# Identity products on TensorE between the first modulation products and at the end of two blocks

## What is computed

```python
def decoder_layer(x, c, S0, u_prev, k_buf, v_buf, pos0, lw):
    mods = (jax.nn.silu(c) @ lw['w_ada'] + lw['b_ada']).reshape(c.shape[0], N_ADA, 1, D_MODEL)
    sh1, sc1, gt1, sh2, sc2, gt2, sh3, sc3, gt3 = [mods[:, i] for i in range(N_ADA)]
    x = x + 0.5 * gt1 * swiglu(modulate(x, lw['norm_ffn1'], sh1, sc1), lw['ffn1_w_gu'], lw['ffn1_w_down'])
    m, st = parallel_heads(modulate(x, lw['norm_mix'], sh2, sc2), u_prev, S0, k_buf, v_buf, pos0, lw)
    x = x + gt2 * m
    x = x + 0.5 * gt3 * swiglu(modulate(x, lw['norm_ffn2'], sh3, sc3), lw['ffn2_w_gu'], lw['ffn2_w_down'])
    return x, st
```

## Time and profile before

| | |
|---|---|
| median of three runs | 2444.17 us |
| time of the profiled execution | 2454.07 us |
| its span, first to last instruction | 2452.3 us |
| TensorE busy | 2363.1 us, 96% of the span |
| VectorE, ScalarE, GpSimd busy | 1107.3, 386.8, 536.3 us |
| mean granted TensorE clock | 0.98 |

### The profile page before, as it was taken

The page is one execution under the profiler, slowest core; times in us unless marked ns, Lnnn a source line. Parts: engine busy times, 40 slices in busy tenths (PEclk is TensorE's granted clock), DMA queues, the critical chain, the costliest instruction groups (busy, mean ns, idle before and its releaser), DMA issues. The chain is left out here.

```text
span 2452.3 us, 50615 instructions
## 1 busy us (share of the span) xinstructions
PE 2363.1 (96%) x21666; PEld 2245.2 (92%) x21666; DVE 1107.3 (45%) x2449; ACT 386.8 (16%) x890; POOL 536.3 (22%) x278
## 2 busy tenths in 40 slices
PE   7899999999999989999989899999999999999997
PEld 5899999999999989888568885999999999999997
DVE  4624443334444364434576665147333444433344
ACT  4100000000000132434621123131000000000003
POOL 3312121212212032111331124313212212121111
PEclk9999999999999999989799999999999999999999
DMA  9232221111011142100320002332111011111102
GB/s 339 86 104 89 82 86 52 50 35 51 17 51 51 45 114 60 36 18 27 113 64 5 4 4 72 108 104 69 52 34 51 17 51 51 51 51 34 51 9 73
DMA packets 162810, 151.22 MB, mean 62 GB/s; under 512 B 21616, under 2 KB 142113, under 8 KB 162264
## 3 DMA queue, kind: packets, MB, share of 16 engines
q1 hardware_dynamic: 162136, 146.75, 19.2%
q10 hardware_dynamic: 144, 2.23, 0.2%
q0 software_dynamic: 384, 0.07, 0.0%
HBM read 137.98 MB, written 11.34 MB: 61 GB/s over the span
## 5 line engine op out<-in xcount | busy, mean ns | idle before, releaser
L516 PE MATMUL bank<-hh,f_up_hi 128*128 128x368 f32 (+1 forms) x2064 | 677.3, 328 | 1.9 <-POOL hl L440 1.0
L518 PE MATMUL bank<-hh,f_up_lo 128*128 128x368 f32 (+1 forms) x2064 | 675.3, 327 | 0.0
L517 PE MATMUL bank<-hl,f_up_hi 128*128 128x368 f32 (+1 forms) x2064 | 674.4, 327 | 0.0
L1291 DVE TENSOR_TENSOR f_prod<-f_silu,bank 128x368 f32<-128x368 f32 x132 | 70.2, 532 | 763.0 <-PE bank L518 758.2
L531 DVE SCALAR_TENSOR_TENSOR x<-bank,mods,x 128x368 f32<-128x368 f32 (+1 forms) x544 | 306.1, 572 | 199.7 <-PE bank L518 186.9
L516 PEld LDWEIGHTS bank<-hh,f_up_hi 128*128 128x128 f32 x2064 | 387.6, 188 | 7.4 <-issue 7.3
L517 PEld LDWEIGHTS bank<-hl,f_up_hi 128*128 128x128 f32 x2064 | 387.8, 188 | 0.0
L518 PEld LDWEIGHTS bank<-hh,f_up_lo 128*128 128x128 f32 x2064 | 387.7, 188 | 0.0
L995 POOL TENSOR_TENSOR f_up_lo<-f_up_raw,f_up_hi 128x2048 fp32r<-128x2048 f32 x44 | 203.2, 4619 | 768.5 <-DVE f_up_hi L1278 768.5
L516 PE MATMUL bank<-f_a_hi,f_dn_hi 128*128 128x368 f32 (+1 forms) x1056 | 347.0, 329 | 0.8 <-DVE f_scratch L534 0.8
L518 PE MATMUL bank<-f_a_hi,f_dn_lo 128*128 128x368 f32 (+1 forms) x1056 | 345.5, 327 | 0.0
(11 more groups left out here) (385 smaller groups left out, 2894.2 us busy)
## 6 DMA issues: line engine op xcount, KB each, us to landing
f_up_raw<-in_ffn_w_gu SPq DMA_DIRECT2D x88, 512.0 KB, 5.0
f_dn_raw<-in_ffn_w_down SPq DMA_DIRECT2D x22, 1024.0 KB, 7.4
late<-in_w_ada SPq DMA_DIRECT2D x12, 1024.0 KB, 4.9
ada<-in_w_ada SPq DMA_DIRECT2D x16, 512.0 KB, 10.9
w_in_raw<-in_w_in SPq DMA_DIRECT2D x16, 512.0 KB
gates<-in_w_ada SPq DMA_DIRECT2D x8, 1024.0 KB, 7.4
x_in<-in_x_prompt SPq DMA_DIRECT2D x8, 512.0 KB, 8.0
ada<-in_w_ada SPq DMA_DIRECT2D x4, 1024.0 KB, 9.9
```

The costliest lines, as they stand in the source:

```text
L516: pe.matmul(out, wh, rh, start=(n == 0), stop=False)
L517: pe.matmul(out, wh, rl, start=False, stop=False)
L518: ins = pe.matmul(out, wl, rh, start=False, stop=(n == last))
L1291: dve.tensor_tensor(prod[u % 2][:, 0:n], silu[u % 2][:, 0:n], k.psum[2 * (u % 2) + 1][:, 0:n], ALU.mult).then_inc(up_free, 1)
```

## The change

A helper issues products of the 128x128 float32 identity with itself into a PSUM bank that nothing reads afterwards. It is called with 8, 8, 10 and 4 products between the four first modulation products and the spreads, with 16 at the end of the first feed-forward's block, and with 20 at the end of the recurrence block. One wait is added ahead of the first modulation product, for VectorE's copy out of the bank that the products write.

```diff
--- before.py
+++ after.py
@@ -509,6 +509,13 @@
                 self.spread(pe, t)
 
 
+def keep_busy(pe, k, bank, n):
+
+    ident = k.c("ident")
+    for _ in range(n):
+        pe.matmul(bank[:, 0:P], ident, ident, start=True, stop=True)
+
+
 def three_passes(pe, out, pairs):
 
     last = len(pairs) - 1
@@ -621,11 +628,16 @@
             turn(j)
         norm.means(pe, 1)
         pe.wait_ge(self.c_done, 1)
+        pe.wait_ge(self.x_high, self.NX - 1)
         self.half_product(pe, 0, 0)
+        keep_busy(pe, k, k.psum[3], 8)
         self.half_product(pe, 0, 1)
         norm.spread(pe, 0)
+        keep_busy(pe, k, k.psum[3], 8)
         self.half_product(pe, 0, 2)
+        keep_busy(pe, k, k.psum[3], 10)
         self.half_product(pe, 0, 3)
+        keep_busy(pe, k, k.psum[3], 4)
         norm.spread(pe, 1)
         ada.turn(pe, 0, self.turned)
         pe.wait_ge(self.par_done, 1)
@@ -1200,6 +1212,7 @@
                     three_passes(pe, out[:, 0:TW], [(hi[:, c], lo[:, c], k.hh[:, c, 0:TW], k.hl[:, c, 0:TW]) for c in range(KD)]
                                  ).then_inc(win.mm_done, 1)
                 mix.means(pe, 2)
+                keep_busy(pe, k, k.psum[6], 16)
 
             if first:
                 pe.sem_inc(late.used, 4)
@@ -2895,6 +2908,7 @@
             for m in range(PAIRS):
                 ins = pe.transpose(k.psum[1][0:HD, P * m:P * m + P], state[:, m], ident)
             ins.then_inc(wkv_turned, 1)
+            keep_busy(pe, k, k.psum[0], 20)
 
         @block.vector
         def _(dve):
```

## The result

The changed kernel took 2452.29 us, the median of 13 runs (2447.23 to 2459.93); the kernel before, timed beside it, 2443.51 us, the median of 13 (2438.44 to 2454.71). The ratio is 1.0033, 95% interval 1.0021 to 1.0044: 8.1 us slower, between 5.1 and 10.8. The time forecast was 2448.0 in a range of 2441 to 2454, so the range holds it; "no difference that can be measured", the likeliest case of the forecast, is wrong.

What follows compares the result with a forecast made beforehand. Long stages were taken as bound by TensorE's products, so only three gaps at half clock could pay: -0.3 + 2.2 + 1.9 = +3.8 us, 2444.17 becoming 2448.0 us, range 2441 to 2454.

Steps and rivals of the forecast that it cites:

- no difference that can be measured: Whole kernel: a change under 0.2% (4.9 us) either way, given a chance of 0.59.
- spare time: Both block ends: TensorE drains before GpSimd, by 0.92 us at the first and 2.43 us at the recurrence's.
- first end: First feed-forward's block end: 16 products delay the block by 2.7 us, a kept clock may save 0.9; taken as +2.2 us.
- recurrence end: Recurrence block's end: 20 products delay it by 3.6 us, output projection at full clock returns 1.7; +1.9 us.
- price of a product: All three places: one identity product takes 0.225 us at full clock, 0.453 at half, judged from the spreads.
- the first place: Kernel start, 8, 8, 10 and 4 products: clock kept up, VectorE gets the turn 0.3 us sooner; -0.3 us.
- the refund: Kernel start: fourth modulation product, spread and turn run at full clock; the fourth takes about 1.07 us, not 1.94.
- the three places don't depend on that: Whole kernel: the profiled execution, 9.9 us above the median, still gives the median's shift, +3.8 us.
- The bound of +1.7: Kernel start: cost in an execution whose clock would not have fallen, turn at 37.56 against 35.85; +1.7 us.
- Rival 1: All three places: products do not hold the clock and cost 0.453 us each; +17.8 us, 2462, chance 0.10.
- Rival 2: Recurrence's end alone stays at half clock until its block is over; sum +9.0 us, 2453.2, chance 0.17.
- Rival 3: All three places: products are cheap, near a transpose's 0.09 us; sum -3.8 us, 2440.4, chance 0.13.

Runs made afterwards that it cites:

- within the slack: Kernel before plus three identity products at the first block's end and four at the recurrence's, none at the start: ratio 0.9992.
- more products: The full change with 56 and 60 products at the two block ends in place of 16 and 20: ratio 1.0089 to the kernel before.

## Why the prediction was right or wrong

**The mechanism at the two block ends was right.** The prediction named who drains last, the spare time of 0.92 and 2.43 us, and that the 16 products push the pause they were to fill. All are in the profile after. Forecast and measured: first end +2.2 and +2.5, recurrence end +1.9 and +1.6. The experiments within the slack and with more products bear the rule out on both sides of the spare time. That the first end costs 0.3 more than forecast fits the spare time, which was taken from the execution with the most of it.

**The price of a product was right, that of a group was left out.** At full clock a product takes 0.225 us as forecast, but each group of them about 0.18 more. In the three groups ahead of the fourth modulation product that is 0.5 us.

**The step that failed is the first place, "-0.3 us, all on the path".** It measures +2.0 in the stage, +2.6 from the first modulation product to the turn. Two things went wrong in it. The overrun was larger by the groups: in the profile after the turn starts at 38.17 and not at 37.56. Above all, the refund was taken from one execution, in which the fourth modulation product ran at half clock, as if that were every execution's: "the three places don't depend on that" is the sentence that does not hold. In six of the seven profiles without products the turn came 9.92 to 10.54 us after the first modulation product, in the one used for the forecast 12.63. The bound of +1.7, for an execution in which the clock had not fallen, described what most executions do, also those in which the clock falls at the second product, and it was dismissed with "the trace shows the other case". So the sum should have been nearer 6 than 3.8, and past the 4.9 us that can be told from nothing.

**The rivals.** Rival 1 (the products do not hold the clock) is out: the clock stood at 1.00 through 24.9 to 38.9 us in the change, and TensorE's 56 products in 12.77 us kept the pace. Its sum was too small besides: it counts 0.453 us only from the ten products on; with the first sixteen at that price too, by the same steps, the turn would start near 47 us and not at 42.5. The argument against it is sound, though the clock column of the earlier trace rows reads 1.00 in both microseconds and its counts are not starts: four transposes start in the first and ten in the second, 0.21 and 0.11 us apart. Rival 2 gave the time that came, +9.0, but not for its reason: the clock climbed within the 20 products in the profile after, and they took 5.87 us, not nine (6.35 and 6.53 in the other two profiles with 20). Rival 3 (products near 0.09 us) is out, with 0.225.

**The range and the chances.** The range held the time because it took in rival 2, whose mechanism did not occur: that is luck and not the sum. The chance of 0.36 for slower was low for the reason above.

## What to carry to other kernels

Products that only keep TensorE's clock up are free exactly where TensorE waits and somebody else sets the end of that wait; count their price against the spare time, and before a point where all engines meet read who drains last first. What they can return is only the half-speed part of the work that follows, and if that work then waits for another engine, the pause has merely moved. A refund that rests on the clock must be read from several executions: one profile shows one of its cases.

## What was not expected of the hardware

- The pauses that drop the clock are not the same from execution to execution. At the start the kernel before had its fourth modulation product at 1.94 us in one profile, while in the other and in three more kernels without products there it was the second. The slow product cost time only where no wait for memory followed that could take it up.
- The stage at the end of the input projection took between 41.7 and 50.1 us with the same instructions, the four longest with TensorE at 1.2 GHz for 27 us on end. It is the largest source of spread between executions that the profiles show, as large as the whole cost of this change.
- A drain of TensorE behind a queue of small products is long (2.17 us at both ends against 0.65 at the first end before), because it begins while its last products still run: at the first end it starts at 880.5 us in the change, and the products end at 878.82 + 3.84 = 882.7. At the recurrence's end, behind four transposes at half clock, it was 2.11 us long before the change as well.
